# Each low part of the gate and up weights that GpSimd makes is written as two subtractions of half the columns

## What is computed

```
xn = rms_norm(x)
q, k, v, hc, gb, gc = split(xn @ w_in)          # attention (3 dilated windows) and a short convolution beside it
h  = x + concat(attention, conv) @ w_out
hn = rms_norm(h)
y  = h + (silu(hn @ w_gate) * (hn @ w_up)) @ w_down     # w_gate, w_up: 1024 x 2816, w_down: 2816 x 1024
out = rms_norm(y)                                # all in float32
```

## Time and profile before

| | |
|---|---|
| median of three runs | 1216.79 us (1215.94 to 1216.95) |
| the profiled execution: time, span | 1217.06 us, 1215.3 us |
| PE busy | 1197.9 us (99%) |
| DVE, POOL, ACT busy | 679.3 us (56%), 509.6 us (42%), 438.1 us (36%) |
| granted clock of PE | full speed (mean 0.999) |
| gate and up stage | about 520 to 965 us |
| low parts of line 966 | 161 instructions: 151 of 512 columns, 8 of 256, 2 of 1024 |

### The profile page before, as it was taken

How to read it: one execution, slowest core, us unless ns; L and a number is a source line. 1 busy time by engine, 2 the same in 40 slices (tenths; PEclk the granted TensorE clock), 3 DMA queues, 4 the chain that set the end, 5 groups by cost and what they waited for, 6 DMA issues and landing times.

```text
span 1215.3 us, 22908 instructions
## 1 busy us (share of the span) xinstructions
PE 1197.9 (99%) x9257; PEld 1136.5 (94%) x9257; DVE 679.3 (56%) x1133; ACT 438.1 (36%) x828; POOL 509.6 (42%) x420
## 2 busy tenths in 40 slices
PE   7999999999999999999999999999999999999998
PEld 6998779889877799999999999999999999999998
DVE  6888214414677623479555444454554178756665
ACT  7111120000378711355443343334333443445452
POOL 3436023233144341052788768776878640000020
PEclk9999999999999999999999999999999999999999
DMA  5478676343223151012614342245444995323223
GB/s 214 156 281 262 230 262 235 139 174 103 84 92 111 48 185 65 1 45 69 241 48 170 116 149 96 106 175 218 166 173 163 345 342 203 94 88 96 86 74 108
DMA packets 70393, 182.66 MB, mean 150 GB/s; under 512 B 7376, under 2 KB 24464, under 8 KB 66320
## 3 DMA queue, kind: packets, MB, share of 16 engines
q1 hardware_dynamic: 70144, 180.92, 42.5%
q10 hardware_dynamic: 144, 0.27, 0.1%
HBM read 136.33 MB, written 44.83 MB: 149 GB/s over the span
## 4 chain that ended last, share of the span: by engine, by line
PE 48%; DVE 2%; POOL 1%; issue 1%; DMA 0%; ACT 0%; DVEq 0%; ACTq 0%
PE ps L1577 9%; PE ps L1579 9%; PE ps L1578 9%; PE ps L1626 6%; PE ps L1627 6%; PE ps L1628 6%; PE ps L1601 1%; PE ps L1600 1%; PE ps L1602 1%; POOL w_lo L966 1%; DVE norms L2735 1%; DMA w_stage<-in_w 0%; DVE combo_b L2262 0%; POOL w_stage L1009 0%; DVE w_lo L2663 0%
## 5 line engine op out<-in xcount | busy, mean ns | idle before, releaser
L1118 PE MATMUL ps<-act_hi,w_hi 128*128 128x352 f32 x480 | 157.4, 328 | 8.2 <-DVE act_lo L2267 8.2
L1577 PE MATMUL ps<-combo,w_hi 128*128 128x264 f32 x544 | 154.9, 285 | 1.7 <-DVE evac L2651 1.2
L1120 PE MATMUL ps<-act_hi,w_lo 128*128 128x352 f32 x480 | 154.8, 323 | 0.0
L1119 PE MATMUL ps<-act_lo,w_hi 128*128 128x352 f32 x480 | 154.7, 322 | 0.0
L1579 PE MATMUL ps<-combo,w_lo 128*128 128x264 f32 x544 | 154.5, 284 | 0.0
L1578 PE MATMUL ps<-combo,w_hi 128*128 128x264 f32 x544 | 154.3, 284 | 0.0
L1626 PE MATMUL ps<-hid,w_hi 128*128 128x264 f32 x536 | 152.7, 285 | 0.0
L1627 PE MATMUL ps<-hid,w_hi 128*128 128x264 f32 x536 | 152.4, 284 | 0.0
L1628 PE MATMUL ps<-hid,w_lo 128*128 128x264 f32 x536 | 152.3, 284 | 0.0
L966 POOL TENSOR_TENSOR w_lo<-w_stage,w_hi 128x512 fp32r<-128x512 f32 (+1 forms) x51 | 76.2, 1495 | 106.1 <-ACT w_hi L1704 106.0
L1577 PEld LDWEIGHTS ps<-combo,w_hi 128*128 128x128 f32 x544 | 102.2, 188 | 2.1 <-issue 1.4
(11 more groups left out here) (470 smaller groups left out, 3237.1 us busy)
## 6 DMA issues: line engine op xcount, KB each, us to landing
w_stage<-in_w SPq DMA_DIRECT2D x56, 512.0 KB, 4.1
resid<-in_state_k SPq DMA_DIRECT2D x8, 1792.0 KB, 11.0
norms<-in_w SPq DMA_DIRECT2D x22, 512.0 KB, 4.4
t_d<-norms SPq DMA_DIRECT2D x11, 1024.0 KB, 4.9
h_d<-evac SPq DMA_DIRECT2D x36, 264.0 KB, 2.3
v_buf<-in_state_v SPq DMA_DIRECT2D x9, 1024.0 KB, 7.0
resid<-in_xT SPq DMA_DIRECT2D x16, 528.0 KB, 7.3
late<-h_d SPq DMA_DIRECT2D x6, 1056.0 KB, 12.9
```

Source lines behind the costliest of these rows:

```text
L1118: pe.matmul(out, hi, rhs_hi, start=first, stop=False)
L1119: pe.matmul(out, hi, rhs_lo, start=False, stop=False)
L1120: return pe.matmul(out, lo, rhs_hi, start=False, stop=last)
L1577: pe.matmul(out, hi[:, wk], x_hi[:, k, tk], start=(k == 0 and first), stop=False, skip_group_check=not first)
```

## The change

`weight_low` wrote a unit's low part with one `tensor_tensor` subtraction over all its columns. It now writes the first half of the columns with one subtraction and the second half with another, and only the second one raises the semaphore `half_split`. The wait ahead of them, the data, the buffers and the order of everything else are the same. Line 966 becomes two instructions: 302 of 256 columns, 16 of 128, 4 of 512, so 161 more in the program.

```
             def weight_low(f, product):
 
                 pool.wait_ge(half_hi, HI_NO[f, product])
-                cols_ = half_slots(f, product)
-                pool.tensor_tensor(w_lo_row[:, cols_], half_unit(f, product), f32(w_hi_row[:, cols_]), ALU.subtract
+                source, lo, hi = half_unit(f, product), *(t[:, half_slots(f, product)] for t in (w_lo_row, w_hi_row))
+                n = source.shape[1] // 2
+                pool.tensor_tensor(lo[:, 0:n], source[:, 0:n], f32(hi[:, 0:n]), ALU.subtract)
+                pool.tensor_tensor(lo[:, n:2 * n], source[:, n:2 * n], f32(hi[:, n:2 * n]), ALU.subtract
                                    ).then_inc(half_split, 1)
```

## The result

Four executions of the changed kernel have a median of 1224.84 us (1222.66 to 1226.65). Four of the kernel before on the same chip have 1216.37 us (1215.80 to 1216.95). The ratio is 1.0069, with a 95% interval from 1.0051 to 1.0086. The change makes the kernel 8.5 us slower. Forecast was 0.9 us, and the measured time lies outside the range. The profiled execution took 1224.68 us, its span is 1222.8 us; before they were 1217.06 and 1215.3 us.

What follows compares the result with a forecast made beforehand. PE, busy 99% of the span, was taken as the bound. 1.17 - 0.29 + 0 + 0 + 0 = +0.88 us on the profiled 1217.06 us gave 1217.94, a median of 1217.7 us; range 1216.2 to 1219.5 us.

Steps and rivals of the forecast that it cites:

- The cost of a split: POOL's low parts: a unit in two halves takes 1.38 us instead of 1.25, 0.13 us more, bounds 0 and 0.19.
- nine splits between 616 and 634 us: POOL's chain from 616.35 us: nine splits delay a raw up load and PE's start at 643.69 by 1.17 us.
- PE's wait of 1.94 us in place of 0.79: Sign expected in the profile after: PE's wait at 643.69 us becomes about 2 us instead of 0.8 us.
- the wait at 581 us: DVE gets in about 0.6 us sooner, so PE's wait at 581.01 us goes: -0.29 us, bounds -0.29 and 0.
- PE never waits for a low part after 650 us: Sign expected in the profile after: no wait of PE for line 966 after 650 us.
- POOL's busy time: Sign expected in the profile after: POOL busy about 20 us more, from 161 splits of 0.13 us.
- The 2.1 us lie beside matmuls, with 3.55 us of room at the tightest place: Later pairs: 16 splits per pair add 2.1 us of POOL time, hidden behind matmuls, costing PE nothing.
- After 643.69 PE has no wait that could take the delay back: PE is busy without a gap to 890 and from 965 to 1200 us, so the earlier delay stays.
- The 0.30 us at 890.46: PE's existing wait there, taken as unchanged: 0 us, bounds -0.3 and +0.65 if five splits delay a raw buffer's load.
- The second rival: Halves each blocked by DVE, loads late in later pairs: 2.2 us at 643.69 plus 1.3 us, +3.5 us, 1220.3 us; chance 0.12.
- At 616.52: PE's wait for DVE's first_hidden of tile 3, at 616.35 us before: change taken as 0, bounds -0.6 and +0.26 us.

Runs made afterwards that it cites:

- experiment 2: Changed kernel's halves only from tile 6 on, whole low parts for tiles 0 to 5: 1222.72 us, ratio 1.0052 against the kernel before.
- 3: Kernel before, low parts whole, with one POOL `memset` of an unread column ahead of each: 1217.34 us, ratio 1.0006 against the kernel before.
- experiment 11: Kernel before, whole low parts, with SP's second gate buffer load moved ahead of the down weights' loads: 1216.90 us, ratio 1.0001.
- experiment 4: Changed kernel, halves kept, with SP's odd gate load moved ahead of load_sums: 1219.81 us, ratio 1.0029 against the kernel before.
- Experiment 5: Kernel before, low parts whole, with five one-column POOL `memset`s ahead of each: 1225.64 us, ratio 1.0073 against the kernel before.
- experiment 10: Kernel before, low parts whole, with three one-column POOL `memset`s ahead of each: 1219.16 us, ratio 1.0021 against the kernel before.
- 12: Changed kernel, halves kept, with DVE's second_gate moved ahead of the next pair's first weight sums: 1224.17 us, ratio 1.0060 against the kernel before.
- 1: Changed kernel's halves only for tiles 0 to 5, whole low parts from tile 6 on: 1218.95 us, ratio 1.0022 against the kernel before.
- 6: Changed kernel with each low part split into seven eighths and one eighth instead of halves: 1228.02 us, ratio 1.0088 against the kernel before.

## Why the prediction was wrong

**Right.** The cost of a split (0.14 us, forecast 0.13); nine splits between 616 and 634 us (1.26 us, forecast 1.17) and PE's wait of 1.94 us in place of 0.79 ("about 2 us instead of 0.8 us"); the wait at 581 us gone. PE never waits for a low part after 650 us, as said. POOL's busy time grew by 32 us rather than 20: 161 x 0.14 = 22.5 us are splits, and the other 9.5 us are what is left of low parts that DVE holds up 15.6 us more than before (below), with the sums and hidden products of lines 1003, 1009 and 1016 held up less. That the wait of 0.79 us grew by just 1.15 us has luck in it. With whole low parts up to there the traces of experiments 2, 3 and 11 have no wait, no wait and 1.15 us at this place, as the load took 5.6, 5.0 and 6.4 us until DVE could start (5.8 before); with one split in every unit it is 1.68 to 1.94 us.

**The step that failed** is "The 2.1 us lie beside matmuls, with 3.55 us of room at the tightest place", and with it "After 643.69 PE has no wait that could take the delay back", where waits were looked for that a delay might shrink and none for what it might start. The 3.55 us are the room between a low part and its product. That room held: nothing in pairs 6 to 18 waits for a low part. But low parts are also what SP waits for before it refills a raw buffer, and that way POOL's room was what it waited ahead of P3's low part, 0.56 to 1.64 us in pairs 8 to 16. The splits of a pair and the longer hold-ups by DVE were more than that. So POOL's lateness went on, by SP's raw load, the store behind it, load_sums, the gate load and ACT back to POOL, and four turns took 41.4 us on average against 40.1 us of PE's pair, where they had taken 40.6. It came out at PE through ACT's copy of P7' and DVE's second_gate, and cost 4.5 us where the sum had zero. Experiment 4 shows the path, since moving one load across the store takes 5.3 us off the changed kernel and, by experiment 11, nothing that can be told off the one before.

A row that pointed to it was in hand. The 0.30 us at 890.46 is a wait for ACT, which had copied from a load that came late; I bounded it at +0.65 us as one place, where the two turns ahead of it had taken 41.7 and 41.4 us.

**The second rival came nearest and had the wrong condition.** It placed the loss in loads that are late in later pairs, at 0.12, but tied it to halves that are each blocked and priced the later pairs at 1.3 us. Experiment 5 reaches the loss with no halves. How much blocking adds beside the split is open: by the line of experiment 10 there is room for it, and also for a steeper curve, and by POOL's busy time there is none. Before, some 48 POOL instructions of line 966 were more than 0.1 us over their usual time, 21.4 us together; after, 55 units, 37.0 us.

**The clock was not thought of.** Behind the 1.94 us wait at 645.15 the first eight matmuls keep their spacing of 0.12 us, then come 16 at 0.22 us with a granted clock of 0.62 over the stretch, that is 1.2 GHz for most of it; 1.54 us are lost. That belongs to the executions rather than to the kernel: after 1.90 (experiment 2), 1.79 and 2.22 us (12) it fell too, after 1.94 (4), 1.92 (5), 1.79 (1), 1.68 (6) and even 3.21 us (12) it did not. What decides between them stays open. It does not make the loss: the two executions of the changed kernel with a mean granted clock of 0.999 and 1.000 took 1226.65 and 1224.99 us.

**At 616.52** PE's wait grew by 0.41 us where I had 0, bounds -0.6 to +0.26. From the operation at 606.93 (line 2641 now) to first_hidden DVE takes 8.55 us (607.13 to 615.68) instead of 8.58, as predicted. The fault lies ahead of it: I had DVE meet PE at 606.93, but the earlier trace rows show no idle time there, and DVE was not waiting. With halves it came to the four operations ahead of that place 0.78 us sooner (603.00 instead of 603.78) and spent 4.13 us on them instead of 3.15, so that it was 0.20 us later, while PE was 0.24 us ahead by the wait that had gone at 581.

## What to carry to other kernels

Room between producer and consumer is not enough for work that is added to an engine in every turn of a steady loop. Ask what else the engine's results release: follow them over the queues that issue loads when they are done, and over stores that stand ahead of those loads, until the work comes back to the engine. The room on that way is the idle time of the engine ahead of the result that releases the load (here 0.56 to 1.64 us), and what is added per turn must fit into it. If it does not, lateness is handed on from turn to turn. The sign in the profile is one wait whose producer started, in successive turns, further apart on average than the period of the bounding engine; one turn alone does not tell, since turns of 38.0 and 41.7 us stood side by side here.

## What the runs showed of the hardware

- Splitting a GpSimd subtraction of 512 columns costs 0.14 us, whether at the half or at seven eighths, and a `memset` of one column ahead of it 0.03 to 0.04 us. These are units that DVE does not hold up. Held-up units of 512 columns mostly start the next one after 1.71 us before, after 1.72 us with five columns of `memset`, and with halves after 1.85 us, or 2.3 us where both halves are held up.
- Three DVE operations in a row on 256 columns of SBUF took 0.95 us each beside half-size POOL operations, where they took 1.51, 0.41 and 0.41 us beside a whole one.
- The clock fell behind idle places of 1.94, 1.90, 1.79 and 2.22 us and did not behind others of 1.94, 1.92, 1.79 and 3.21 us. A fall cost about 1.5 us (16 matmuls at 0.22 instead of 0.12 us in the changed kernel, 15 in experiment 2).
- The store of 1 MB was issued 0.37 us behind a raw weight load in pair 14 instead of 1.28 us, and it was 7.60 us instead of 7.02 until SP could go on. From issue to landing the eleven have a median of 6.5 us instead of 4.9. In experiment 4 it is 6.8 us, which costs nothing there, as no gate load stands behind the store.
